# Final norm of a two-layer backbone: transposing before the root is known, and storing in half tiles

## The chip, the cores and the metric

The kernel runs on one core of a Trainium2 chip. The core has TensorE (PE, the matrix engine), VectorE (DVE), ScalarE (ACT), GpSimd (POOL) and SyncE (SP), each with its own instruction stream; they are ordered by semaphores alone. SP issues all transfers between memory (DRAM) and the on-chip SBUF. They run on 16 DMA engines. TensorE writes its results to PSUM, eight banks of 512 fp32 numbers in each of 128 partitions. The metric is the time of one execution on the device in microseconds (us).

## The reference

Two streams of tokens, 512 latent and 128 context tokens with 1024 channels each, pass through two layers (attention of several kinds, then a gated MLP). The change touches only what comes after the second layer:

```python
def rmsnorm(x, g):
    xf = x.astype(jnp.float32)
    y = xf * lax.rsqrt(jnp.mean(xf * xf, axis=-1, keepdims=True) + EPS)
    return (y * g.astype(jnp.float32)).astype(x.dtype)
...
    y_prompt = rmsnorm(xp, final_norm)
    y_sample = rmsnorm(xs, final_norm)
```

Each token's row is divided by the root of its mean square (the "root" below is the reciprocal of that root, one number per token) and multiplied by a weight per channel. Everything is fp32.

## The kernel before

The state X is kept transposed: channels on the partitions, tokens along the free dimension. X has KT = 8 tiles of 128 channels, each with T = 644 columns: 512 latent tokens, 2 zero columns, 128 context tokens, 2 zero columns. There are TT = 5 token tiles of 128, starting at the columns TILE0. The outputs have tokens as rows, so the end needs 5 x 8 transposes of 128 x 128 blocks, done on TensorE with the identity matrix (line 1149 in the profile, helper `tr`).

The order of the work is written out by hand for each engine. Semaphores count up over the whole program. The names that matter at the end of the second layer (DEPTH = 2):

- TensorE ends the MLP with the down products for channel tiles 4 to 7, each into two PSUM banks. DVE adds each to X (`add_products`, line 1699) and counts x_fin up, tile by tile. The earlier part of the residual was added to X from the buffer DN (`residual`, counted by x_pre).
- ACT squares each finished tile (`square`, line 905), DVE sums the squares over tiles into SUM (`add_square`, lines 1632 and 1635, counted by ss_add).
- `statistics` on TensorE sums SUM over the channels into five columns of bank 5 (st_mm). DVE makes the mean squares out of them (`norm_start`, line 1642, nv), POOL raises them to the power -0.5 (`norm_root`, line 847, rv). NS holds both.
- In the version before, DVE then puts each token's root on the diagonal of a tile (DG, line 1645), TensorE spreads these over all partitions into banks 6 and 7 (`spread_roots`), DVE multiplies X by them into XN (`normalise`, lines 1656 and 1657, two buffers), ACT multiplies by the norm's weight FN into YO (line 1132, counted by fin_y), TensorE transposes, and two engines copy out of PSUM into OUT: DVE the first 512 channels of a token tile (line 1604, fin_ev[0]), ACT the second 512 (line 885, fin_ev[1]). SP sends a token tile when both halves are there (line 821).

The same functions `norm_start` and `normalise` serve the four norms inside the layers.

SBUF space is reused by stages. YO and OUT lie over buffers of the MLP: CF, G_hi and G_lo take the first 12 T columns of that region, DN the 8 T behind them.

Of the kernel before, what the change touches and what calls it, by code (L numbers as in the profile page):

```python
# [17 lines left out]
F32 = mybir.dt.float32  # L18
F32R = mybir.dt.float32r
ACT = mybir.ActivationFunctionType  # L20
ALU = mybir.AluOpType
# [3 lines left out]
P = 128  # L25
D = 1024
DEPTH = 2
KT = D // P
NLAT, NCTX = 512, 128
QT = NLAT // P  # L30
CTX0 = NLAT + 2
T = CTX0 + NCTX + 2
HALF = 384
TILE0 = [P * i for i in range(QT)] + [CTX0]
TT = QT + 1
# [5 lines left out]
EPS = 1e-6  # L41
# [271 lines left out]
def backbone_program(nc, x_prompt, x_sample, cache_mla_ckv, cache_mla_kpe, cache_gqa_k, cache_gqa_v,  # L313
# [5 lines left out]
    with ctx:  # L319
        def sb(name, shape, dt=F32, stack=ctx):  # L320
            return stack.enter_context(nc.sbuf_tensor(name, shape, dt))

        def sem(name):
# [3 lines left out]
        X = sb("X", [P, KT, T])  # L327
# [10 lines left out]
        NS = sb("NS", [P, 2, 8])  # L338
        FN = sb("FN", [P, KT])
# [17 lines left out]
        t = ExitStack()  # L357
# [11 lines left out]
        XN = sb("XN", [P, 2, T], F32, b)  # L369
# [16 lines left out]
        a = ExitStack()  # L386
# [4 lines left out]
        t = ExitStack()  # L391
        KS = sb("KS", [P, TT + 1, 4, P], F32, t)
        t.close()
        t = ExitStack()
# [4 lines left out]
        t = ExitStack()  # L399
# [6 lines left out]
        a = ExitStack()  # L406
# [6 lines left out]
        a = ExitStack()  # L413
# [5 lines left out]
        a = ExitStack()  # L419
# [3 lines left out]
        AS0 = sb("AS0", [P, NAS, D], F32, a)  # L423
        a.close()
        a = ExitStack()
        YO = sb("YO", [P, KT, T], F32, a)
        OUT = sb("OUT", [P, TT, D], F32, a)
        a.close()
        b.close()

        PS = ctx.enter_context(nc.psum_tensor("PS", [P, 8, 512], F32))
# [5 lines left out]
        aw_used, x_pre = sem("aw_used"), sem("x_pre")  # L437
# [7 lines left out]
        sq_done, ss_add, st_mm, nv, rv, dg, bc_mm = (sem(n) for n in (  # L445
            "sq_done", "ss_add", "st_mm", "nv", "rv", "dg", "bc_mm"))
        xn, hf, h_hi, h_lo = sem("xn"), sem("hf"), sem("h_hi"), sem("h_lo")
# [11 lines left out]
        new_out, x_mid, x_fin = sem("new_out"), sem("x_mid"), sem("x_fin")  # L459
# [3 lines left out]
        fin_y, fin_tr, y_out = sem("fin_y"), sem("fin_tr"), sem("y_out")  # L463
        fin_ev = [sem("fin_ev_dve"), sem("fin_ev_act")]

        block = ctx.enter_context(nc.Block())

        def staged(l, x):

# [188 lines left out]
        def _(sp):  # L658
# [41 lines left out]
            for l in range(DEPTH):  # L700
# [40 lines left out]
                for r in range(NATTADA + NPROJ + NOUT):  # L741
                    kind, n = RAW_KIND[r]
# [3 lines left out]
                    elif n < NTOKEN:  # L746
                        ch, k, kn = TOKEN_ITEMS[n]
                        c0, w = TOKEN_CHUNKS[ch]
                        src = w_in[bass.ds(l, 1), P * k:P * (k + kn), c0:c0 + w]
                    elif n < NPROJ:  # L750
                        c0 = FEAT_CHUNKS[ch - NTOKEN // 2]
# [6 lines left out]
                    if kind == "w" and n >= NPROJ and kh == 1:  # L758

                        for g, a in [(g, a) for g in range(2) for a in range(2)]:  # L760
                            r0 = 512 + 256 * g + P * a
                            rows = w_out[l, r0:r0 + P, 256 * ch:256 * (ch + 1)]
                            dst = RW[HD * a:HD * (a + 1), ring(l, r), 512 * g:512 * (g + 1)]
# [51 lines left out]
                        stage_ada(l + 1, x)  # L815
            sp.wait_ge(new_out, 96 * DEPTH)
            for i in range(TT):
                sp.wait_ge(fin_ev[0], i + 1)
                sp.wait_ge(fin_ev[1], i + 1)
                dst = y_sample[0, P * i:P * (i + 1), :] if i < QT else y_prompt[0, :, :]  # L820
                sp.dma_start(dst, OUT[:, i, :]).then_inc(y_out, 16)
            sp.wait_ge(y_out, 16 * TT)

# [57 lines left out]
        def _(act):  # L883
            def copy(dst, src):
                return nc.scalar.activation(dst, src, ACT.Copy)  # L885
# [48 lines left out]
            for l in range(DEPTH):  # L934
# [21 lines left out]
                for ch in range(len(TOKEN_CHUNKS)):  # L956
# [4 lines left out]
                    dst, w = (PMG, PMM, PMS)[ch], TOKEN_CHUNKS[ch][1]  # L961
                    for i in range(TT):
# [5 lines left out]
                        if ch == 1:  # L968
                            ins = copy(dst[:, i, 0:w], of)
                        else:  # L970
                            copy(dst[:, i, 0:256].rearrange("p (j a n) -> p a j n", j=2, a=2),
                                 of[:, 0:256].rearrange("p (a j n) -> p a j n", j=2, a=2))
                            ins = copy(dst[:, i, 256:w], of[:, 256:w])
# [4 lines left out]
                for o in range(2):  # L978
                    for dst, src in zip(pieces(GC[:, o, :]), halves(o)):
                        ins = copy(dst, src)  # L980
# [142 lines left out]
                    act_pairs(m)  # L1123


            for t in range(KT):
                act.wait_ge(x_fin, DEPTH * KT + t + 1)
                square(2 * DEPTH, t)
            for t in range(KT):
                act.wait_ge(xn, 2 * DEPTH * KT + t + 1)  # L1130
                for c0, c1 in ((0, NLAT), (CTX0, CTX0 + NCTX)):
                    ins = nc.scalar.activation(YO[:, t, c0:c1], XN[:, t % 2, c0:c1], ACT.Copy,
                                               scale=FN[:, t:t + 1])
                ins.then_inc(fin_y, 1)
            for i in range(TT):
                act.wait_ge(fin_tr, TT + i + 1)
                copy(OUT[:, i, 512:D], PS[:, i, :]).then_inc(fin_ev[1], 1)

# [2 lines left out]
        def _(pe):  # L1143
# [3 lines left out]
            def tr(out, in_):  # L1147
                n = in_.shape[0]
                return nc.tensor.transpose(out, in_, K[0:n, K_ID:K_ID + n])  # L1149
# [3 lines left out]
            for i in range(TT):  # L1153
                pe.wait_ge(x_in[i], 16)
                for hb in range(2):
                    n = 2 * i + hb
                    if n >= 6:
                        pe.wait_ge(x_ev, n - 5)
                    for t in range(4):
                        ins = tr(PS[:, n % 6, P * t:P * (t + 1)], XIN[:, i, P * (4 * hb + t):P * (4 * hb + t + 1)])  # L1160
# [32 lines left out]
            def statistics(N):  # L1193

                pe.wait_ge(ss_add, N * 7 + 7)
                for i in range(TT):
                    ins = mm(PS[:, 5, i:i + 1], SUM[:, TILE0[i]:TILE0[i] + P], ONES[:, 0:1], True, True)
                ins.then_inc(st_mm, 1)

            def spread_roots(N):  # L1200

                for i in range(TT):
                    pe.wait_ge(dg, N * TT + (i + 1))
                    out = PS[:, 6, P * i:P * (i + 1)] if i < QT else PS[:, 7, 0:P]
                    ins = mm(out, ONES, DG[:, i, :], True, True)
                ins.then_inc(bc_mm, 1)
# [10 lines left out]
            for l in range(DEPTH):  # L1217
# [11 lines left out]
                for x in range(8 * ADA_A):  # L1229
                    rows, landed_, value = staged(l, x)  # L1230
# [16 lines left out]
                for s, (ch, k0, kn) in enumerate(TOKEN_ITEMS):  # L1247
                    w = TOKEN_CHUNKS[ch][1]
                    w_ready(s)
                    for kk in range(kn):  # L1250
# [3 lines left out]
                        for i in range(TT):  # L1254
# [4 lines left out]
                            c0 = TILE0[i]  # L1259
# [4 lines left out]
                            ins = mm(out, H_lo[:, k, c0:c0 + P], whi, False, k == KT - 1)  # L1264
# [4 lines left out]
                for f in range(3):  # L1269
                    for kh in range(2):  # L1270
# [6 lines left out]
                        for kk in range(4):  # L1277
                            for o in range(2):
                                pair = (o, 2 + o, o)[f]
                                ins = three(halves(pair), wslot(l, s), 2 * P * kk + P * o,  # L1280
                                            (H_hi[:, 4 * kh + kk, :], H_lo[:, 4 * kh + kk, :]),
                                            kh == 0 and kk == 0, kh == 1 and kk == 3)
# [277 lines left out]
                for t in range(4):  # L1560
                    pe.wait_ge(up_ev, l * 44 + (40 + t + 1))
                    for kc in range(2):
                        ins = gated_product(t, wslot(l, NW - 4), PAIRS % 2, kc, kc == 0, False)
                ins.then_inc(w_used, 1)
                pe.wait_ge(w_lo, l * NW + (RAW + NW - 2))
                for kc in range(2):
                    pe.wait_ge(g_lo, l * 22 + 21 + kc)
                    for t in range(4):
                        ins = gated_product(t, wslot(l, NW - 3), (PAIRS - 1) % 2, kc, False, kc == 1)
# [4 lines left out]
                for t in range(4):  # L1574
                    pe.wait_ge(x_fin, (l + 1) * KT + (t + 1))
                    for p in range(2):
                        ins = gated_products(t, wslot(l, NW - 2 + p), (PAIRS - 2 + p) % 2, p == 0, p == 1)
# [3 lines left out]
                        ins.then_inc(dn_mm, 1)  # L1581


            statistics(2 * DEPTH)
            spread_roots(2 * DEPTH)
            for n in range(2 * TT):
                hb, i = divmod(n, TT)
                if i == 0:
                    pe.wait_ge(fin_y, 4 * hb + 4)
                if hb:  # L1590
                    pe.wait_ge(fin_ev[0], i + 1)
                for t in range(4):
                    ins = tr(PS[:, i, P * t:P * (t + 1)], YO[:, 4 * hb + t, TILE0[i]:TILE0[i] + P])
                ins.then_inc(fin_tr, 1)

# [2 lines left out]
        def _(dve):  # L1600
            v = nc.vector

            def copy(dst, src):
                return v.tensor_copy(dst, src)
# [12 lines left out]
            for n in range(2 * TT):  # L1617
                dve.wait_ge(x_tr, n + 1)
                c0, hb = TILE0[n // 2], n % 2
                ins = copy(X[:, 4 * hb:4 * hb + 4, c0:c0 + P], PS[:, n % 6, :].rearrange("p (t n) -> p t n", n=P))  # L1620
# [7 lines left out]
            def add_square(N, t):  # L1628
# [4 lines left out]
                else:  # L1633
                    dve.wait_ge(ss_add, N * 7 + (t - 1))
                    v.tensor_tensor(SUM[:, :], SUM[:, :], SQ[:, t % 2, :], ALU.add).then_inc(ss_add, 1)

            def norm_start(N):

                v.memset(HF[:, :, NLAT:CTX0], 0.0)
                v.memset(HF[:, :, T - 2:T], 0.0)  # L1640
                dve.wait_ge(st_mm, N + 1)
                v.tensor_scalar(NS[:, 0, 0:TT], PS[:, 5, 0:TT], 1.0 / D, EPS, ALU.mult, ALU.add).then_inc(nv, 1)
                dve.wait_ge(rv, N + 1)
                for i in range(TT):
                    v.tensor_scalar(DG[:, i, :], IDENT, NS[:, 1, i:i + 1], None, ALU.mult).then_inc(dg, 1)
                for t in range(2):
                    normalise(N, t)

            def normalise(N, t):
                if t < 2:  # L1650
                    dve.wait_ge(bc_mm, N + 1)
                elif N == 2 * DEPTH:
                    dve.wait_ge(fin_y, t - 1)
                else:
                    dve.wait_ge(hf, N * (2 * KT) + (2 * t - 2))
                v.tensor_tensor(XN[:, t % 2, 0:NLAT], X[:, t, 0:NLAT], PS[:, 6, :], ALU.mult)  # L1656
                v.tensor_tensor(XN[:, t % 2, CTX0:CTX0 + P], X[:, t, CTX0:CTX0 + P], PS[:, 7, 0:P],
                                ALU.mult).then_inc(xn, 1)
# [44 lines left out]
            for l in range(DEPTH):  # L1703
# [36 lines left out]
                for t in range(TT):  # L1740
                    r = SS[:, 1, 6 * t:6 * t + 6].rearrange("p (h o) -> p h o", o=1).to_broadcast([P, 6, HD])
                    qk = PMG[:, t, 0:384].rearrange("p (h n) -> p h n", n=HD)
                    ins = v.tensor_tensor(qk, qk, r, ALU.mult)
# [279 lines left out]
                assert own.n == DVE_OWN, own.n  # L2023

            add_square(2 * DEPTH, KT - 1)
            norm_start(2 * DEPTH)
            for t in range(2, KT):
                normalise(2 * DEPTH, t)
            for i in range(TT):
                dve.wait_ge(fin_tr, i + 1)  # L2030
                copy(OUT[:, i, 0:512], PS[:, i, :]).then_inc(fin_ev[0], 1)


# [52 lines left out]
```

## Time and profile before

| | |
|---|---|
| Median of 3 runs | 1773.33 us (1772.14 to 1773.69) |
| Profiled execution | 1772.28 us |
| Its span | 1770.4 us |
| TensorE busy | 1676.5 us, 95% of the span |
| Last matrix product of the second layer | issued at 1742.87 us |
| First output transfer issued | 1762.18 us |
| Output | 5 transfers of 512 KB, 2.62 MB |

The span runs from the first to the last event of the core in the trace, and the execution's own time is 1.88 us longer. Times below are counted from the span's start. A timeline row names the start, the duration, the engine, the line, the operation and "out<-in" with the shapes; several of one kind in a row are merged, with their count, and the duration is that of the whole row. In brackets stands how long the engine had been idle and what ended that.

### The profile page before, as it was taken

Reading aid. Unit: us, or ns where it says so; the run is one execution under the profiler, and the core shown is the slowest. Engines: PE = TensorE matmul, PEld = TensorE weight load, DVE = VectorE, ACT = ScalarE, POOL = GpSimd, SP = SyncE. Lnnn points to the kernel's source line nnn. Section 1 sums busy time; section 2 is a strip of 40 time slices with the busy share of each in tenths; the row PEclk is TensorE's granted clock in tenths of the full one; section 3 lists DMA queues with packets and bytes.
Section 4 is the critical chain, followed back from the end, with each engine's and each line's share of the span. In section 5 each row is a group of like instructions: output and inputs, shape, how many; then the busy total and the mean of one; then the engine's idle time right before and its main releaser. Section 6 shows DMA issues by size and latency. Waiting matters only on the chain.

```text
span 1770.4 us, 29691 instructions
## 1 busy us (share of the span) xinstructions
PE 1676.5 (95%) x11702; PEld 1511.6 (85%) x11702; DVE 1011.8 (57%) x1647; ACT 597.2 (34%) x1109; POOL 542.9 (31%) x297
## 2 busy tenths in 40 slices
PE   6999998998999999999989999899799999999996
PEld 4888555798999999999968965569799999999996
DVE  4275445236766666666834744442576666666675
ACT  3423444425222222222342244452432222222223
POOL 1354010222433334333325500113233334443340
PEclk7999999998999999999999999999899999999998
DMA  8323541121222222222443245202122222222211
GB/s 320 106 72 91 169 129 38 42 67 48 78 77 71 71 71 71 74 80 72 175 149 95 60 151 154 86 25 60 37 72 73 82 72 71 71 77 77 84 48 60
DMA packets 147730, 156.17 MB, mean 88 GB/s; under 512 B 8201, under 2 KB 118325, under 8 KB 147637
## 3 DMA queue, kind: packets, MB, share of 16 engines
q1 hardware_dynamic: 147636, 154.87, 28.2%
q8 instruction: 66, 1.08, 0.3%
q14 instruction: 28, 0.22, 0.0%
HBM read 151.54 MB, written 3.31 MB: 87 GB/s over the span
## 4 chain that ended last, share of the span: by engine, by line
PE 61%; issue 20%; POOL 9%; ACT 4%; DVE 3%; DMA 1%; SPq 1%; POOLq 0%; ACTq 0%; DVEq 0%
PE PS L1145 56%; POOL W_lo L839 8%; PE PS L1149 5%; ACT HF L913 1%; ACT PT L885 1%; POOL SS L855 1%; DMA AS<-in_w_ada_dram 1%; ACT PR L1019 1%; DMA BS_N<-in_w_ada_dram 0%; ACT W_hi L885 0%; ACT H_hi L885 0%; ACT PMM L885 0%; DVE HO L1873 0%; DVE H_lo L1663 0%; DVE XN L1656 0%
## 5 line engine op out<-in xcount | busy, mean ns | idle before, releaser
L839 POOL TENSOR_TENSOR W_lo<-RW,W_hi 128x1024 fp32r<-128x1024 f32 (+1 forms) x184 | 482.6, 2632 | 939.7 <-ACT W_hi L885 939.7
L1145 PE MATMUL PS<-H_hi,W_hi 128*128 128x384 f32 x1856 | 577.6, 311 | 12.2 <-DVE H_lo L1663 7.9
L1145 PE MATMUL PS<-H_hi,W_lo 128*128 128x384 f32 x1856 | 578.1, 311 | 0.0
L1145 PE MATMUL PS<-H_lo,W_hi 128*128 128x384 f32 x1856 | 578.0, 311 | 0.0
L1145 PEld LDWEIGHTS PS<-H_hi,W_hi 128*128 128x128 f32 x1856 | 353.6, 190 | 13.6 <-issue 13.5
L1145 PEld LDWEIGHTS PS<-H_hi,W_lo 128*128 128x128 f32 x1856 | 352.1, 190 | 0.0
L1145 PEld LDWEIGHTS PS<-H_lo,W_hi 128*128 128x128 f32 x1856 | 351.9, 190 | 0.1
L885 ACT ACTIVATE W_hi<-RW 128x1024 fp32r<-128x1024 f32 (+1 forms) x184 | 191.2, 1047 | 100.6 <-PE PS L1145 100.6
L1145 PE MATMUL PS<-G_hi,W_hi 128*128 128x384 f32 x704 | 218.7, 311 | 2.2 <-DVE G_lo L1936 2.2
L1145 PE MATMUL PS<-G_lo,W_hi 128*128 128x384 f32 x704 | 218.1, 310 | 0.0
L1145 PE MATMUL PS<-G_hi,W_lo 128*128 128x384 f32 x704 | 217.9, 310 | 0.0
L885 ACT ACTIVATE U<-PS 128x384 f32<-128x384 f32 (+1 forms) x176 | 67.2, 434 | 386.0 <-PE PS L1145 385.7
L1926 DVE SCALAR_TENSOR_TENSOR CF<-U,VT,CF 128x644 f32<-128x644 f32 x88 | 189.1, 2149 | 10.2 <-DVE CF L1923 2.4
L1921 DVE TENSOR_SCALAR CF<-U,VT 128x644 f32<-128x644 f32 x88 | 51.3, 582 | 240.3 <-ACT U L885 239.8
L1923 DVE SCALAR_TENSOR_TENSOR CF<-U,VT,CF 128x644 f32<-128x644 f32 x88 | 138.8, 1577 | 10.3 <-DVE CF L1921 2.4
L1949 DVE TENSOR_TENSOR DN<-PS,DN 128x384 f32<-128x384 f32 (+1 forms) x288 | 120.9, 478 | 25.8 <-PE PS L1145 25.8
L1145 PEld LDWEIGHTS PS<-G_hi,W_hi 128*128 128x128 f32 x704 | 132.8, 189 | 2.6 <-DVE G_lo L1936 2.6
L1145 PEld LDWEIGHTS PS<-G_hi,W_lo 128*128 128x128 f32 x704 | 133.7, 190 | 0.0
L1145 PEld LDWEIGHTS PS<-G_lo,W_hi 128*128 128x128 f32 x704 | 132.6, 188 | 0.0
L885 ACT ACTIVATE G_hi<-CF 128x644 fp32r<-128x644 f32 x44 | 32.7, 744 | 238.2 <-DVE CF L1932 238.2
L1145 PE MATMUL PS<-W_hi,H_hi 128*128 128x512 f32 (+1 forms) x240 | 90.9, 379 | 9.7 <-DVE H_lo L1663 7.4
L885 ACT ACTIVATE PT<-PS 128x512 f32<-128x512 f32 (+1 forms) x102 | 53.9, 577 | 112.7 <-PE PS L1149 108.6
(188 smaller groups left out, 1901.9 us busy)
## 6 DMA issues: line engine op xcount, KB each, us to landing
RW<-in_w_up_dram SPq DMA_DIRECT2D x88, 512.0 KB, 3.7
RW<-in_w_ada_dram SPq DMA_DIRECT2D x64, 512.0 KB, 4.0
RW<-in_w_down_dram SPq DMA_DIRECT2D x44, 512.0 KB, 3.6
RW<-in_w_in_dram SPq DMA_DIRECT2D x28, 512.0 KB, 3.7
AS<-in_w_ada_dram SPq DMA_DIRECT2D x16, 512.0 KB, 11.7
RW<-in_w_out_dram SPq DMA_DIRECT2D x32, 128.0 KB, 3.0
RW<-in_w_out_dram SPq DMA_DIRECT2D x8, 512.0 KB, 3.5
BS_N<-in_w_ada_dram SPq DMA_DIRECT2D x8, 512.0 KB, 7.5
```

Of the source, the lines that this page charges most:

```text
L839: nc.gpsimd.tensor_tensor(W_lo[:, slot, 0:width], RW[:, raw, 0:width], W_hi[:, slot, 0:width].bitcast(F32), ALU.subtract).then_inc(w_lo, 1)
L855: nc.gpsimd.tensor_tensor(SS[:, 1, 0:40], SS[:, 0, 0:40], K[:, K_MH:K_MH + 40], ALU.pow).then_inc(hp, 1)
L885: return nc.scalar.activation(dst, src, ACT.Copy)
L913: nc.scalar.activation(HF[:, t % 2, c0:c1], XN[:, t % 2, c0:c1], ACT.Identity, bias=MOD[:, 24 * w + t, cond:cond + 1], scale=AB[:, w, t, c ...
L1019: nc.scalar.activation(prob_ap(step, u), score_ap(step, u), ACT.Exp, bias=stat(step, 0, u), scale=scale, accum_out=stat(step, 1, u)).then_ ...
L1145: return nc.tensor.matmul(out, lhsT, rhs, start=start, stop=stop, skip_group_check=True)
L1149: return nc.tensor.transpose(out, in_, K[0:n, K_ID:K_ID + n])
L1921: v.tensor_scalar(CF[:, ch, s, :], U[:, ch, s, 0:T], column(0), None, ALU.mult).then_inc(cv_own, 1)
L1923: v.scalar_tensor_tensor(CF[:, ch, s, :], U[:, ch, s, 1:T + 1], column(1), CF[:, ch, s, :], ALU.mult, ALU.add).then_inc(cv_own, 1)
L1926: v.scalar_tensor_tensor(CF[:, ch, s, :], U[:, ch, s, 2:T + 2], column(2), CF[:, ch, s, :], ALU.mult, ALU.add).then_inc(cv_done, 1)
L1949: ins = v.tensor_tensor(out, src, out, ALU.add)
```

## The change

The final norm is written out in another order. ACT multiplies each tile of X by the norm's weight, right after squaring it, into YO. TensorE transposes those tiles without the root: the first 512 channels of all five token tiles before `statistics`, the second 512 after it, in the banks that `final_bank` names. The root, one number per token, is applied by DVE and ACT while they copy a transposed tile (now with tokens on the partitions) out of PSUM. `spread_roots`, DG, XN and the products that filled it are gone from the final norm, and the mean squares have a function of their own, `roots`, which `norm_start` calls too. SP sends each half of a token tile by itself: ten transfers of 256 KB with rows of 2 KB in place of five of 512 KB with rows of 4 KB. YO and OUT change places in SBUF, so that YO lies over DN and OUT over CF and G_hi. ACT waits for x_pre before it writes YO.

```diff
@@ memory @@
+        OUT = sb("OUT", [P, TT, D], F32, a)
+        sb("beside_output", [P, 12 * T - TT * D], F32, a)
         YO = sb("YO", [P, KT, T], F32, a)
-        OUT = sb("OUT", [P, TT, D], F32, a)
...
+        def final_bank(hb, i):
+
+            return (6, 7, 5, 0, 1)[i] if hb else i
@@ SP @@
             for i in range(TT):
-                sp.wait_ge(fin_ev[0], i + 1)
-                sp.wait_ge(fin_ev[1], i + 1)
-                dst = y_sample[0, P * i:P * (i + 1), :] if i < QT else y_prompt[0, :, :]
-                sp.dma_start(dst, OUT[:, i, :]).then_inc(y_out, 16)
-            sp.wait_ge(y_out, 16 * TT)
+                rows = y_sample[0, P * i:P * (i + 1), :] if i < QT else y_prompt[0, :, :]
+                for hb in range(2):
+                    sp.wait_ge(fin_ev[hb], i + 1)
+                    sp.dma_start(rows[:, 512 * hb:512 * (hb + 1)],
+                                 OUT[:, i, 512 * hb:512 * (hb + 1)]).then_inc(y_out, 16)
+            sp.wait_ge(y_out, 32 * TT)
@@ ACT @@
+            act.wait_ge(x_pre, DEPTH * KT)
             for t in range(KT):
                 act.wait_ge(x_fin, DEPTH * KT + t + 1)
                 square(2 * DEPTH, t)
-            for t in range(KT):
-                act.wait_ge(xn, 2 * DEPTH * KT + t + 1)
-                for c0, c1 in ((0, NLAT), (CTX0, CTX0 + NCTX)):
-                    ins = nc.scalar.activation(YO[:, t, c0:c1], XN[:, t % 2, c0:c1], ACT.Copy,
-                                               scale=FN[:, t:t + 1])
-                ins.then_inc(fin_y, 1)
+                nc.scalar.activation(YO[:, t, :], X[:, t, :], ACT.Copy, scale=FN[:, t:t + 1]).then_inc(fin_y, 1)
+            act.wait_ge(rv, 2 * DEPTH + 1)
             for i in range(TT):
                 act.wait_ge(fin_tr, TT + i + 1)
-                copy(OUT[:, i, 512:D], PS[:, i, :]).then_inc(fin_ev[1], 1)
+                nc.scalar.activation(OUT[:, i, 512:D], PS[:, final_bank(1, i), :], ACT.Copy,
+                                     scale=NS[:, 1, i:i + 1]).then_inc(fin_ev[1], 1)
@@ TensorE @@
+            def final_rows(hb, i):
+
+                for t in range(4):
+                    ins = tr(PS[:, final_bank(hb, i), P * t:P * (t + 1)], YO[:, 4 * hb + t, TILE0[i]:TILE0[i] + P])
+                ins.then_inc(fin_tr, 1)
+            pe.wait_ge(fin_y, 4)
+            for i in range(TT):
+                pe.wait_ge(x_fin, DEPTH * KT + 5 + i // 2)
+                final_rows(0, i)
             statistics(2 * DEPTH)
-            spread_roots(2 * DEPTH)
-            for n in range(2 * TT):
-                hb, i = divmod(n, TT)
-                if i == 0:
-                    pe.wait_ge(fin_y, 4 * hb + 4)
-                if hb:
-                    pe.wait_ge(fin_ev[0], i + 1)
-                for t in range(4):
-                    ins = tr(PS[:, i, P * t:P * (t + 1)], YO[:, 4 * hb + t, TILE0[i]:TILE0[i] + P])
-                ins.then_inc(fin_tr, 1)
+            pe.wait_ge(fin_y, KT)
+            for i in range(TT):
+                if i == 2:
+                    pe.wait_ge(nv, 2 * DEPTH + 1)
+                elif i > 2:
+                    pe.wait_ge(fin_ev[0], i - 2)
+                final_rows(1, i)
@@ DVE @@
+            def roots(N):
+
+                dve.wait_ge(st_mm, N + 1)
+                v.tensor_scalar(NS[:, 0, 0:TT], PS[:, 5, 0:TT], 1.0 / D, EPS, ALU.mult, ALU.add).then_inc(nv, 1)
...
             add_square(2 * DEPTH, KT - 1)
-            norm_start(2 * DEPTH)
-            for t in range(2, KT):
-                normalise(2 * DEPTH, t)
+            roots(2 * DEPTH)
+            dve.wait_ge(rv, 2 * DEPTH + 1)
             for i in range(TT):
                 dve.wait_ge(fin_tr, i + 1)
-                copy(OUT[:, i, 0:512], PS[:, i, :]).then_inc(fin_ev[0], 1)
+                v.tensor_scalar(OUT[:, i, 0:512], PS[:, final_bank(0, i), :], NS[:, 1, i:i + 1], None,
+                                ALU.mult).then_inc(fin_ev[0], 1)
```

## Rows read from the trace of the kernel before

**Rows 1.** The page: one engine's busy time, and the DMA queue's packets.
```profile
PE 1676.5 (95%) x11702; PEld 1511.6 (85%) x11702; DVE 1011.8 (57%) x1647; ACT 597.2 (34%) x1109; POOL 542.9 (31%) x297
...
q1 hardware_dynamic: 147636, 154.87, 28.2%
```

**Rows 2.** Timeline of the end, from the last down product on.
```profile
1742.87 0.28 PE L1145 MATMUL PS<-G_hi,W_lo 128*128 128x256 f32 x1
1743.19 1.14 DVE L1699 SCALAR_TENSOR_TENSOR X<-PS,MOD,X 128x384 f32<-128x384 f32 x3 [1.68 <-PE PS L1145]
1744.24 1.75 DVE L1635 TENSOR_TENSOR SUM<-SUM,SQ 128x644 f32<-128x644 f32 x2
1744.36 0.74 ACT L905 ACTIVATE SQ<-X 128x644 f32<-128x644 f32 x1 [2.81 <-DVE X L1699]
...
1746.05 1.27 PE L1145 MATMUL PS<-K,SUM 128*128 128x1 f32 x10 [2.90 <-DVE SUM L1635]
1747.36 0.16 DVE L1642 TENSOR_SCALAR NS<-PS 128x5 f32<-128x5 f32 x1 [1.34 <-PE PS L1145]
1747.60 1.16 POOL L847 TENSOR_TENSOR NS<-NS,K 128x5 f32<-128x5 f32 x1 [19.97 <-DVE NS L1642]
1748.80 1.07 DVE L1645 TENSOR_SCALAR DG<-K,NS 128x128 f32<-128x128 f32 x5 [1.28 <-POOL NS L847]
...
1752.61 7.83 ACT L1132 ACTIVATE YO<-XN,FN 128x512 f32<-128x512 f32 x16 [7.51 <-DVE XN L1657]
...
1756.55 6.66 PE L1149 MATMUL PS<-K,YO 128*128 128x128 f32 x40 [4.90 <-ACT YO L1132]
...
1762.18 4.16 SPq L821 DMA_DIRECT2D out_dram<-OUT  x5
```

**Rows 3.** Stretches with the DMA share and GB/s last; packets of 33 to 36.
```profile
1762.60:1763.00 0.40, 0.40 (x6) 0.37 (x4) 0.00 (x0) 0.40 (x2) 0.00 (x0) 1.00 0.00 0
1763.00:1763.40 0.40, 0.21 (x2) 0.00 (x0) 0.00 (x0) 0.40 (x2) 0.00 (x0) 1.00 0.98 399
...
1769.20:1769.60 0.40, 0.00 (x0) 0.00 (x0) 0.00 (x0) 0.00 (x0) 0.00 (x0) 0.50 0.75 287
...
33.00:36.00 3.00, 2.72 (x34) 1.01 (x34) 1.77 (x5) 0.21 (x1) 0.00 (x0) 0.88 0.98 380
...
DMA packets 594, 1.14 MB, mean 380 GB/s; under 512 B 37, under 2 KB 37, under 8 KB 594
```

**Rows 4.** Groups by line and shape, ACT: a scaled and a plain copy.
```profile
L1132 ACT ACTIVATE YO<-XN,FN 128x512 f32<-128x512 f32 x8 | 5.7, 714 | 7.7 <-DVE XN L1657 7.5
...
L885 ACT ACTIVATE H_hi<-HO 128x512 fp32r<-128x512 f32 x12 | 7.6, 631 | 9.9 <-DVE HO L1873 9.9
```

**Rows 5.** Timeline of ACT and DVE while the last down products run.
```profile
1732.53 1.14 DVE L1699 SCALAR_TENSOR_TENSOR X<-PS,MOD,X 128x384 f32<-128x384 f32 x3 [0.40 <-PE PS L1145]
...
1736.09 1.14 DVE L1699 SCALAR_TENSOR_TENSOR X<-PS,MOD,X 128x384 f32<-128x384 f32 x3 [1.68 <-PE PS L1145]
...
1737.25 0.75 ACT L905 ACTIVATE SQ<-X 128x644 f32<-128x644 f32 x1 [2.81 <-DVE X L1699]
```

**Rows 6.** Stretches: length, busy PE, PEld, DVE, ACT, POOL; granted clock; DMA share, GB/s.
```profile
1743.20:1746.00 2.80, 0.00 (x0) 0.00 (x0) 2.70 (x7) 0.74 (x1) 0.00 (x0) 1.00 0.00 0
...
1756.50:1759.30 2.80, 2.75 (x13) 2.75 (x14) 2.59 (x8) 2.71 (x6) 0.00 (x0) 0.50 0.00 0
...
1761.50:1764.00 2.50, 1.71 (x16) 1.47 (x14) 0.87 (x2) 2.50 (x5) 0.00 (x0) 1.00 0.42 162
```

**Rows 7.** Instructions of the tile OUT: ns min/median/max, first and last start.
```profile
L1604 DVE COPY OUT<-PS x5: 679/679/683, 1759.3 to 1761.7; 128x512 f32<-128x512 f32 x5
L885 ACT ACTIVATE OUT<-PS x5: 592/607/632, 1761.5 to 1763.4; 128x512 f32<-128x512 f32 x5
L821 SPq DMA_DIRECT2D out_dram<-OUT x5: 356/608/1153, 1762.2 to 1765.2; - x5
...
DMA to landing us min/median/max: 2.7/4.2/4.8
```

More of the change, by code:

```diff
@@ L1640, in norm_start @@
                 v.memset(HF[:, :, T - 2:T], 0.0)
-                dve.wait_ge(st_mm, N + 1)
-                v.tensor_scalar(NS[:, 0, 0:TT], PS[:, 5, 0:TT], 1.0 / D, EPS, ALU.mult, ALU.add).then_inc(nv, 1)
+                roots(N)
                 dve.wait_ge(rv, N + 1)
@@ L1651, in normalise @@
                     dve.wait_ge(bc_mm, N + 1)
-                elif N == 2 * DEPTH:
-                    dve.wait_ge(fin_y, t - 1)
                 else:
```

## The prediction

> **What bounds the kernel now.** The page comes first. TensorE is busy for 95% of the span [rows 1], so almost everywhere only work taken off TensorE would count. The end is different, and the change lies there. The timeline of the end is read next. The last down product is issued at 1742.87 us. From there to the span's end at 1770.4 no matrix work of the layers is left, and each step waits for the one before [rows 2]. Read it as a relay. DVE adds the last residual tile (1743.19) and the last squares. TensorE sums over channels (1746.05). DVE turns the sums into mean squares (1747.36), and POOL raises them to the power -0.5 from 1747.60 for 1.16 us. Only then, at 1748.80, does the old normalisation start: the diagonal tiles DG, their spreading, 16 products on DVE beside 16 scaled copies on ACT (7.83 us from 1752.61), 40 transposes (6.66 us from 1756.55), copies out, and at 1762.18 the first output transfer. So 1762.18 - 1748.80 = 13.38 us pass between "the roots are there" and "the first byte may leave".
>
> The stretches of the DMA engines are read last. They stand at 0.00 until 1763.00, are at 0.98 right after, and are still at 0.75 in the last stretch with data, 1769.20 to 1769.60 [rows 3]. From its first issue on, the output phase is bound by bytes: 2.62 MB (5 x 128 rows x 4 KB) at 399/0.98 = 407 GB/s take 6.44 us. The issue adds 0.82 us in front, and some 0.9 us lie behind the data.
>
> **The change, part by part.** *Scaled copies moved ahead of the roots.* ACT makes YO from X itself, one copy of 644 columns per tile, each behind that tile's square. Such a copy of 512 columns takes 714 ns [rows 4]; scaled by columns this is 0.90 us at most. A tile comes every 3.55 us (DVE's adds at 1732.53 and 1736.09), and ACT sits idle for 2.81 us before a square [rows 5]. I cost the copies at nothing: that idle time hides them. For the first tiles, which come closer together, a square may end some 0.3 us later. DVE has 0.40 us of slack before the add at 1732.53 and 1.68 before the next [rows 5]. Without any cover the eight copies would cost 8 x 0.90 = 7.2 us. The new ACT wait for x_pre has only squares queued behind it, and they need tiles that DVE updates after those residuals, in program order. The last square (1744.36) stands before the last copy, so the sums keep their time. The copy ends by 1744.36 + 0.74 + 0.90 = 1746.0, before the sums over channels are done.
>
> *Twenty transposes ahead of the sums.* TensorE now transposes the first half of all five token tiles between its last product and the statistics. Their inputs (YO 0 to 3, residual tiles up to 6) are ready by then. At full clock 16 transposes took 1.71 us, 0.107 each; at half clock 13 took 2.75, 0.212 each [rows 6]. The granted clock of 1743.20 to 1746.00 is 1.00, right after products without a gap [rows 6]. So I take 0.107: 20 x 0.107 = 2.14 us from about 1743.2 to 1745.3, inside the old wait until 1746.05. Cost nothing, with 0.7 us to spare; at half clock they would end at 1747.4 and make the sums 1.4 us late. Those sums are what is queued behind them.
>
> *Second half of the transposes.* They follow the sums, from about 1747.3. Tiles 0 and 1 need no bank back, tile 2 waits for DVE's read of bank 5 (1747.52), tiles 3 and 4 for DVE's first and second copy out. Tile 3 would be ready near 1750.0 (half clock: 1750.4) and ACT gets to its fourth copy at about 1750.5: nothing, or a few tenths behind the transfers.
>
> *Taken out:* DG, its spreading, the 16 products, two clears of HF and the old copies. They are the 13.38 us. In their place stands one copy out that multiplies by the token's root. A plain DVE copy of this shape took 679 ns with starts 0.60 apart, ACT's 607 ns and 0.48 [rows 7]. The trace has no such DVE multiply that reads PSUM. Bounds: 0.68 us as the copy, and 1.07 for five multiplies of 128 columns [rows 2], which makes 1.07 x 4 / 5 = 0.86 for 512. I take 0.68, as shape and source are those of the copy. For ACT, a scale from memory makes 714 instead of 631 ns from SBUF [rows 4], so about 0.69 from PSUM. Ten halves are then ready between 1749.5 and 1751.9, 256 KB per 0.30 us, twice as fast as the engines can carry them.
>
> *First issue.* DVE starts at 1748.80 and ends at 1749.48. SP issued 0.07 us after ACT's first copy before (1761.50 + 0.61 to 1762.18), so 1749.55 instead of 1762.18: a gain of 12.63 us.
>
> *Ten half transfers.* The bytes stay and the rows become 2 KB. Stores of 2 KB rows aren't in the trace. The nearest is a load: in 33 to 36 us, 594 packets with 37 small ones carry 1.14 MB, 2 KB each, at 380 GB/s for a share of 0.98 [rows 3], 388 GB/s. The far bound is the whole queue's mean, 154.87 MB in 28.2% of the span [rows 1], 310 GB/s at 1 KB a packet. 2.62 MB take 6.76 us at 388 and 8.45 at 310, against 6.44 now: a loss of 0.3 (taken) to 2.0 us. A rule of the Trainium skill would make even this 0.3 nothing: "DMA: Bandwidth & Descriptors", Specifications, asks for only 512 B per transfer to reach line rate, so the sum would be 12.6; the rows of this trace, which differ between 2 KB and 4 KB, decide for 12.3.
>
> SP needs ten issues instead of five. One takes 356 ns at the least and 608 in the median, and the longest, 1153, belong to a full queue [rows 7]. A half needs 0.68 us of transfer and the next issue is there after 0.43 to 0.68 us (0.07 between two), so the engines stay fed, just so at the upper value. Nothing else is queued on SP. Its waits alternate between DVE's and ACT's half of a tile; both are ahead of it after the first.
>
> **The sum.** 12.63 - 0.32 = 12.3 us. The profiled execution took 1772.28 us for its span of 1770.4, so 1760.0. It lies 1.05 below the median of the runs, 1773.33, so the time to expect is 1773.33 - 12.3 = 1761.0 us.
>
> **Rivals.** *Stores of half rows are slower, or the issues limit.* For it: the queue's 310 GB/s, and issues of 0.61 us. Against it: the 2 KB loads at 388. Price 8.45 - 6.76 = 1.7 us: 1762.7.
>
> *The moved transposes hold up the sums.* The clock falls by 1743 or they start late. For it: 0.50 in 1756.50 to 1759.30, after gaps. Against it: 1.00 in the very stretch. Price 1.4 us: 1762.4.
>
> *The early copies aren't hidden.* ACT's eight copies delay squares, DVE's sums wait for squares, DVE's adds stand behind the sums, and TensorE's last products wait for freed banks. For it: that chain of waits exists. Against it: 2.81 and 1.68 us of idle time per tile. In full 7.2 us: 1768.2.
>
> *Slower than before: the ten transfers go one behind the other.* Each 256 KB would cost a whole landing, which is 2.7 us at the least for an output transfer of today [rows 7]; SP's queue is the place. End: 1749.55 + 27 + some 0.4 = 1776.95, that is 1773.33 + 6.5 = 1779.9. It decides from (12.63 + 1770.4 - 1762.18)/10 = 2.1 us per half. Against it: the five transfers of today are issued within 3.0 us [rows 7] and all their bytes pass between 1763.0 and 1769.6 [rows 3], where five landings of 2.7 us in a row would be 13.5, so they overlap. The Trainium skill speaks for this rival: "DMA: Bandwidth & Descriptors", Rules for kernel authors, asks for 1 MiB or more per DMA, and its fit of about 2.0 us fixed plus bytes at 436 GB/s makes an estimate of 2.6 us per half, 26 us in a row; that fit is for transfers issued by GpSimd, and the overlap in this trace goes against adding it up.
>
> **How the numbers follow.** Forecast 0.70, half rows 0.17, held-up sums 0.06, uncovered copies 0.04, transfers in a row 0.03. The predicted time is the forecast's, 1761.0. The three runs lie from 1.2 below to 0.4 above their median. The range starts at 1761.0 - 0.3 - 1.2 = 1759.5 (no loss by half rows) and ends at 1762.7 + 0.4 = 1763.1, which takes in the half rows and the held-up sums. What a measurement can tell from no change is about 0.2%, 3.5 us: the first three cases are faster, and the fourth in full by 5.1 us. Faster 0.95; same 0.02, for uncovered copies that also hold TensorE; slower 0.03.
>
> **What the profile will show.** Scaled copies between the squares, and DVE's adds at an unchanged pace of 3.55 us; twenty transposes of about 0.11 us behind the last product; the sums over channels starting 3.2 us after that product, as now; DVE's first copy out some 0.04 us behind POOL's root and of 0.68 us; SP's first issue 0.8 us after the root; ten issues; the DMA engines full for some 6.8 us; the end some 8.5 us after the first issue. I am wrong if the first issue comes later than 1750.5, or if the phase behind it is much over 8.5 us: by the first a relay step is new, by the second half rows cost more than 2 KB loads let me think.

## The result, and the profile after

The change took 1760.64 us in the median of four runs (1760.21 to 1761.42), against 1773.51 for the kernel before (four runs, three of them those of the table above): a ratio of 0.993 with a 95% interval of 0.9918 to 0.9942. The forecast was 1761.0. The profiled execution took 1760.21 us for a span of 1758.2, which is 12.2 us below the span before; the sum had been 12.3. Of all runs in this document one, of the kernel called "five whole again" below, took 3945.34 us; it stands in none of the medians.

The timeline of the end, to be laid beside [rows 2], names start, duration, engine, line and operation as there.

```profile
1742.79 0.28 PE L1149 MATMUL PS<-G_hi,W_lo 128*128 128x256 f32 x1
...
1742.92 2.34 PE L1153 MATMUL PS<-K,YO 128*128 128x128 f32 x20
1743.12 1.14 DVE L1711 SCALAR_TENSOR_TENSOR X<-PS,MOD,X 128x384 f32<-128x384 f32 x3 [1.68 <-PE PS L1149]
1744.17 1.75 DVE L1645 TENSOR_TENSOR SUM<-SUM,SQ 128x644 f32<-128x644 f32 x2
1744.28 0.74 ACT L911 ACTIVATE SQ<-X 128x644 f32<-128x644 f32 x1 [2.08 <-DVE X L1711]
1744.93 0.82 ACT L1136 ACTIVATE YO<-X,FN 128x644 f32<-128x644 f32 x1
...
1745.97 1.28 PE L1149 MATMUL PS<-K,SUM 128*128 128x1 f32 x10 [0.71 <-DVE SUM L1645]
...
1747.11 1.51 PE L1153 MATMUL PS<-K,YO 128*128 128x128 f32 x12
1747.29 0.16 DVE L1650 TENSOR_SCALAR NS<-PS 128x5 f32<-128x5 f32 x1 [1.37 <-PE PS L1149]
1747.53 1.17 POOL L853 TENSOR_TENSOR NS<-NS,K 128x5 f32<-128x5 f32 x1 [19.94 <-DVE NS L1650]
1748.73 3.00 ACT L1140 ACTIVATE OUT<-PS,NS 128x512 f32<-128x512 f32 x5 [2.98 <-POOL NS L853]
1748.73 3.38 DVE L2042 TENSOR_SCALAR OUT<-PS,NS 128x512 f32<-128x512 f32 x5 [1.28 <-POOL NS L853]
...
1749.54 1.32 PE L1153 MATMUL PS<-K,YO 128*128 128x128 f32 x8 [0.92 <-DVE OUT L2042]
1749.56 5.86 SPq L826 DMA_DIRECT2D out_dram<-OUT  x10
```

The relay up to POOL's root stands where it stood, 0.07 us earlier as a whole. Behind the root, everything from the diagonal tiles to the plain copies out has given way to one scaled copy: DVE and ACT start their copies at 1748.73, and SP issues at 1749.56, not 1762.18. Twenty transposes sit in the gap before the sums, which wait 0.71 us where they had waited 2.90.

The instructions of the tile OUT answer to [rows 7], the stretches to [rows 3] and [rows 6].

```profile
L826 SPq DMA_DIRECT2D out_dram<-OUT x10: 357/600/645, 1749.6 to 1754.8; - x10
L1140 ACT ACTIVATE OUT<-PS,NS x5: 682/688/705, 1748.7 to 1751.0; 128x512 f32<-128x512 f32 x5
L2042 DVE TENSOR_SCALAR OUT<-PS,NS x5: 741/741/750, 1748.7 to 1751.4; 128x512 f32<-128x512 f32 x5
...
DMA to landing us min/median/max: 2.0/3.0/3.1
```

```profile
1743.10:1745.90 2.80, 2.16 (x20) 1.92 (x18) 2.68 (x5) 1.46 (x2) 0.00 (x0) 1.00 0.00 0
...
1749.50:1750.30 0.80, 0.76 (x5) 0.53 (x6) 0.80 (x2) 0.80 (x2) 0.00 (x0) 1.00 0.00 0
...
1750.30:1757.40 7.10, 0.55 (x4) 0.31 (x4) 1.81 (x3) 1.43 (x3) 0.00 (x0) 0.59 1.00 369
...
1757.40:1757.60 0.20, 0.00 (x0) 0.00 (x0) 0.00 (x0) 0.00 (x0) 0.00 (x0) 0.50 0.01 0
```

The DMA engines are full (share 1.00) from 0.8 us behind the first issue until 0.8 us before the end. Ten transfers are issued between 1749.6 and 1754.8 and overlap. So of the phase from first issue to end, 1758.2 - 1749.56 = 8.64 us, 7.10 us are bytes, as 6.60 of the 8.22 us before were:

```profile
1763.00:1769.60 6.60, 0.21 (x2) 0.00 (x0) 0.00 (x0) 1.05 (x3) 0.00 (x0) 0.85 1.00 397
```

### The profile page after: what moved, and what is told of

It reads as the page before. It is cut to its first block, busy times and chain, and to the rows that moved or that the text cites. A ratio compares the mean times of both kernels' runs of the same rounds, so it can differ in the third digit from the quotient of the medians.

```text
span 1758.2 us, 29644 instructions
## 1 busy us (share of the span) xinstructions
PE 1672.2 (95%) x11692; PEld 1509.4 (86%) x11692; DVE 1004.4 (57%) x1624; ACT 596.0 (34%) x1101; POOL 543.4 (31%) x297
## 4 chain that ended last, share of the span: by engine, by line
PE 62%; issue 20%; POOL 9%; ACT 4%; DVE 3%; DMA 1%; SPq 1%; POOLq 0%; DVEq 0%; ACTq 0%
PE PS L1149 57%; POOL W_lo L845 8%; PE PS L1153 4%; ACT PT L891 1%; POOL SS L861 1%; DMA AS<-in_w_ada_dram 1%; ACT HF L919 1%; ACT PR L1025 1%; DMA BS_N<-in_w_ada_dram 0%; ACT H_hi L891 0%; ACT W_hi L891 0%; ACT PMM L891 0%; DVE HO L1885 0%; DVE H_lo L1675 0%; DVE CF L1935 0%
## 5 line engine op out<-in xcount | busy, mean ns | idle before, releaser
L1149 PE MATMUL PS<-H_hi,W_hi 128*128 128x384 f32 x1856 | 578.0, 311 | 12.2 <-DVE H_lo L1675 7.9
L1935 DVE SCALAR_TENSOR_TENSOR CF<-U,VT,CF 128x644 f32<-128x644 f32 x88 | 140.9, 1601 | 10.3 <-DVE CF L1933 2.4
```

What stands on the lines that cost most here:

```text
L1149: return nc.tensor.matmul(out, lhsT, rhs, start=start, stop=stop, skip_group_check=True)
L1935: v.scalar_tensor_tensor(CF[:, ch, s, :], U[:, ch, s, 1:T + 1], column(1), CF[:, ch, s, :], ALU.mult, ALU.add).then_inc(cv_own, 1)
```

## The experiments

One number serves all of them. The same work does not reach its last stage at the same instant in every execution: in the kernels whose code up to there is the same, DVE's last residual addition starts between 1741.27 and 1745.10 us. This scatter is part of every time, but not of what follows that addition: the change, measured twice, takes 15.08 and 15.01 us from there to the end. The table therefore measures from the addition's start: to the first issue, then to the span's end (the phase).

| kernel | median us (runs) | ratio to before, interval | last addition | to first issue | phase | both |
|---|---|---|---|---|---|---|
| before | 1773.51 (4) | | 1743.19 | 18.99 | 8.22 | 27.21 |
| the change | 1760.64 (4) | 0.993, 0.9918 to 0.9942 | 1743.12 | 6.44 | 8.64 | 15.08 |
| five whole transfers | 1759.85 (4) | 0.9928, 0.9909 to 0.9947 | 1741.44 | 6.43 | 8.23 | 14.66 |
| split alone | 1772.99 (10) | 0.9997, 0.9987 to 1.0007 | 1745.46 | 17.90 | 10.04 | 27.94 |
| transposes late | 1760.45 (4) | 0.9927, 0.991 to 0.9945 | 1741.50 | 6.45 | 8.55 | 15.00 |
| token halves | 1764.56 (4) | 0.9953, 0.9935 to 0.9972 | 1742.66 | 6.43 | 12.11 | 18.54 |
| copies uncovered | 1766.68 (5) | 0.9965, 0.9951 to 0.9979 | 1743.50 | 12.24 | 8.56 | 20.80 |
| quarter rows | 1762.87 (2) | 0.994, 0.992 to 0.996 | 1741.27 | 6.45 | 11.68 | 18.13 |
| even and odd | 1761.11 (2) | 0.993, 0.991 to 0.995 | 1743.99 | 6.43 | 9.28 | 15.71 |
| sums early | 1758.71 (4) | 0.9919, 0.9902 to 0.9935 | 1742.42 | 5.54 | 8.24 | 13.78 |
| sums early, zeroed | 1758.41 (5) | 0.9921, 0.9908 to 0.9933 | 1741.66 | 5.54 | 8.20 | 13.74 |
| the change again | 1761.09 (5) | 0.9935, 0.9922 to 0.9948 | 1744.09 | 6.45 | 8.56 | 15.01 |
| five whole again | 1761.07 (5) | 0.9929, 0.9916 to 0.9942 | 1745.10 | 6.43 | 8.17 | 14.60 |

The theory is the prediction's: a first issue one copy behind the root, then 0.8 us, the bytes at the rate of their row length, and 0.8 to 0.9 us behind them.

**Five whole transfers: undoing one part.** Only SP's loop goes back:

```diff
-                rows = ...
-                for hb in range(2):
-                    sp.wait_ge(fin_ev[hb], i + 1)
-                    sp.dma_start(rows[:, 512 * hb:512 * (hb + 1)], ...)
+                sp.wait_ge(fin_ev[0], i + 1)
+                sp.wait_ge(fin_ev[1], i + 1)
+                dst = ...
+                sp.dma_start(dst, OUT[:, i, :]).then_inc(y_out, 16)
```

> Everything of the change but the transfers: five of 512 KB again. Theory (first issue one copy out behind the root, then bytes at the rate of the row length): both halves of tile 0 are ready at 1749.5, so the first issue stays at 1749.56, and the phase from there to the span's end falls from 8.64 us to the 8.22 of before: time 1760.2. Rival (the half tiles are part of the gain, since the first bytes are ready sooner): first issue and end later by half a tile's transfer, 0.65 us or more: 1761.3 or more.

The first issue stays (6.43 us behind the addition) and the phase falls to 8.23 us. The stretch with data:

```profile
1748.70:1755.30 6.60, 0.47 (x4) 0.23 (x3) 1.73 (x3) 1.35 (x3) 0.00 (x0) 0.59 1.00 397
```

The engines are just as full (1.00) and carry 397 GB/s in rows of 4 KB, where the change carries 369 in rows of 2 KB. So cutting the tiles costs 0.4 us here and brings nothing: ACT's first copy ends before DVE's, and the first whole tile is ready no later than the first half.

**Split alone: the other part.** The kernel before with the new SP loop.

> The kernel before with only its output cut into ten half transfers. Theory: the first half leaves at 1760.05 instead of 1762.18, but the second still waits for ACT's first copy out at 1762.11; one half gone early (0.68 us) less the slower 2 KB rows (0.4): 0.3 us earlier, time 1773.2. Rival (smaller transfers are worth what they start earlier): 2.1 us earlier, 1771.4.

The median is 0.5 us below before, within what can be told from nothing. In this execution the sums over channels took 2.29 us, at a granted clock of 0.50, instead of 1.27, so the two kernels are best laid together at POOL's root (1750.90 here, 1747.60 before): the first issue follows after 12.46 us against 14.58, the end after 22.5 against 22.8. One half leaves 2.1 us early, and the rest waits for ACT. This theory held; nearly all of the gain comes from the other part.

**Transposes late.** All forty behind the sums, a tile's two halves together; DVE's and ACT's waits follow the new order:

```diff
-            pe.wait_ge(fin_y, 4)
+            statistics(2 * DEPTH)
+            pe.wait_ge(fin_y, KT)
             for i in range(TT):
                 pe.wait_ge(x_fin, DEPTH * KT + 5 + i // 2)
                 final_rows(0, i)
-            statistics(2 * DEPTH)
-            pe.wait_ge(fin_y, KT)
-            for i in range(TT):
                 if i == 2:
...
                 final_rows(1, i)
```

> The change, with all forty transposes behind the sums over channels, in pairs of halves. Theory: the root takes POOL from 1747.5 to 1748.7 anyway, and tile 0 is transposed by 1748.1 at full clock, so the first issue stays at 1749.56; 1760.6 if TensorE keeps its full clock, and up to 1761.5 if it falls to half after the gap before the sums (a tile then takes 1.7 us and the transfers starve a little). Rival (moving twenty transposes ahead of the sums is itself worth their 2.1 us): 1762.7.

The first issue is at 6.45 us, as in the change, and both together take 15.00. Timeline and two stretches:

```profile
1744.36 1.28 PE L1149 MATMUL PS<-K,SUM 128*128 128x1 f32 x10 [2.90 <-DVE SUM L1643]
1745.50 6.23 PE L1153 MATMUL PS<-K,YO 128*128 128x128 f32 x40
...
1747.00:1749.00 2.00, 2.00 (x11) 2.00 (x10) 1.41 (x2) 1.37 (x2) 0.08 (x1) 0.50 0.09 36
1749.00:1751.00 2.00, 2.00 (x16) 2.00 (x15) 1.29 (x2) 0.80 (x2) 0.00 (x0) 0.77 1.02 379
```

Even with the clock at half (0.50) from 1747 to 1749, the transposes stay ahead of the transfers: the DMA engines are full (1.02) right after. So placing them ahead of the sums is not what brings the gain. That they no longer need the root is enough: POOL's root and then the transfers cover them. What the place does change is the granted clock: in the change it stays at 1.00 from 1743.1 to 1751.0, here it falls to 0.50 after the gap of 2.90 us and the sums. In split alone it was at 0.50 already while the sums ran behind such a gap, and that cost 1 us. Whether the early place spares an execution this now and then was not tested.

**Token halves.** Ten transfers of 64 tokens by 4 KB rows, to tell row length from the number of issues:

```diff
+                sp.wait_ge(fin_ev[0], i + 1)
+                sp.wait_ge(fin_ev[1], i + 1)
...
-                    sp.wait_ge(fin_ev[hb], i + 1)
-                    sp.dma_start(rows[:, 512 * hb:512 * (hb + 1)],
...
+                    sp.dma_start(rows[64 * hb:64 * (hb + 1), :],
+                                 OUT[64 * hb:64 * (hb + 1), i, :]).then_inc(y_out, 16)
```

> The change with ten transfers of 64 tokens by 4 KB rows in place of 128 tokens by 2 KB. Theory (row length sets the rate): the phase from first issue to the end is 8.2 us as with five transfers, time 1760.2. Rival (ten issues cost it): 8.6 us as in the change, time 1760.6. The phase in the profile decides, since the times lie close together.

Theory and rival both missed: the phase is 12.11 us. **Even and odd** asks whether that is due to 64 rows or to half of the partitions; the slices are `hb:P:2` on both sides.

> As the run with ten transfers of 64 tokens by 4 KB rows, which had a phase of 12.1 us, but with the even and the odd token rows of a tile instead of its lower and its upper half. If half a tile was slow because it reads only one half of the partitions, the phase falls to 8.2 to 8.6 us, time 1760.2 to 1760.6; if any transfer of 64 rows is slow, it stays near 12 us, time 1764.5.

Stretches of the lower and upper halves first, then of the even and odd rows:

```profile
1753.00:1755.00 2.00, 0.00 (x0) 0.00 (x0) 0.00 (x0) 0.00 (x0) 0.00 (x0) 0.54 0.82 262
1755.00:1757.00 2.00, 0.00 (x0) 0.00 (x0) 0.00 (x0) 0.00 (x0) 0.00 (x0) 0.50 0.84 285
```

```profile
1750.40:1751.50 1.10, 1.09 (x8) 0.84 (x8) 1.10 (x2) 1.10 (x3) 0.00 (x0) 1.00 0.00 0
...
1752.00:1754.00 2.00, 0.00 (x0) 0.00 (x0) 0.99 (x2) 0.60 (x2) 0.00 (x0) 0.88 1.01 404
...
1758.30:1759.70 1.40, 0.00 (x0) 0.00 (x0) 0.00 (x0) 0.00 (x0) 0.00 (x0) 0.50 0.02 6
```

Spread over all partitions, rows of 4 KB pass at 404 GB/s although there are ten issues of 256 KB; the change, with as many issues of that size, has 379 to 385 in the middle of its transfers. So the rate does follow the row length, and a transfer of 64 neighbouring partitions pays for its partitions (262 and 285 GB/s, and engines that aren't full). The phase of even and odd, 9.28 us, still missed the 8.2 to 8.6 expected, mainly because 1.1 us lie ahead of the data and 1.4 behind it, where the change has 0.8 and 0.8. Why these two are longer is open, and so is what limits the half of the partitions.

**Quarter rows.** Twenty transfers of 128 tokens by 1 KB.

> The change with twenty transfers of 128 tokens by 1 KB rows. Theory (bytes at the rate of the row length, 310 GB/s at 1 KB by the whole queue's mean): a phase of 10.3 us from first issue to end, time 1762.3. Rival (the issues bind once they are smaller): twenty issues of 0.45 to 0.6 us make 9 to 12 us before the last landing of 2.0, a phase of 11.5 to 14, time 1763.5 to 1766. Rival (row length costs nothing): 8.2 to 8.6, time 1760.6.

The instructions of OUT, and one stretch:

```profile
L826 SPq DMA_DIRECT2D out_dram<-OUT x20: 332/445/492, 1747.7 to 1757.2; - x20
...
DMA to landing us min/median/max: 1.7/1.8/2.1
...
1752.00:1756.00 4.00, 0.00 (x0) 0.00 (x0) 0.00 (x0) 0.00 (x0) 0.00 (x0) 0.50 0.78 259
```

The engines are full for 0.78 only and each transfer lands after 1.8 us (3.0 in the change), so nothing queues there. Issues come (1757.2 - 1747.7)/19 = 0.50 us apart, and they bind: the phase is 11.68 us, as the rival on the issues had it (the theory's 10.3 missed). The median of the two runs, 1762.87 us, lies below that rival's range of times; with two runs and the scatter above it decides nothing. In the change the issues come (1754.8 - 1749.6)/9 = 0.58 us apart, but 256 KB need (7.10 us)/10 = 0.71, so there the bytes bind.

**Copies uncovered.** ACT makes the eight scaled copies behind the eighth square:

```diff
                 square(2 * DEPTH, t)
+            for t in range(KT):
                 nc.scalar.activation(YO[:, t, :], X[:, t, :], ACT.Copy, scale=FN[:, t:t + 1]).then_inc(fin_y, 1)
```

> The change with ACT's eight scaled copies behind all eight squares instead of between them, so that nothing hides them. Theory: copies of 0.82 us, started some 0.72 apart, run from 1745 to 1750.8; the twenty first transposes can start with the fourth copy at 1748.0 and TensorE's sums stand behind them, at 1750.2 at full clock and up to 1752.3 at half; the first issue moves by 4.2 to 6.4 us: 1764.9 to 1767.0. Rival (the copies' place doesn't matter, POOL's root and the transfers cover them): 1760.6.

Timeline, then a stretch:

```profile
1745.31 5.87 ACT L1137 ACTIVATE YO<-X,FN 128x644 f32<-128x644 f32 x8
...
1748.35 4.07 PE L1154 MATMUL PS<-K,YO 128*128 128x128 f32 x20 [4.89 <-ACT YO L1137]
1752.26 1.17 PE L1150 MATMUL PS<-K,SUM 128*128 128x1 f32 x10
...
1748.30:1752.40 4.10, 4.05 (x23) 4.05 (x23) 0.00 (x0) 2.89 (x4) 0.00 (x0) 0.58 0.00 0
```

The first issue moves by 12.24 - 6.44 = 5.8 us, within the 4.2 to 6.4 expected. In the change the sums over channels start 1745.97 - 1743.12 = 2.85 us behind DVE's last addition, which would be 1746.35 here. The transposes that stand before them wait for the copies until 1748.35: 2.0 us. Then TensorE, after an idle gap of 4.89 us, makes the twenty transposes at a mean clock of 0.58, in 4.07 us instead of 2.34, and the sums start at 1752.26: another 3.9 us. So with this order on TensorE the cover of the copies is worth nearly half the gain of the change. What uncovered copies would cost if the sums stood first, no run shows.

**A shorter way to the root.** With the transfers back to five, what is left to shorten is the way to the root. The last experiments let DVE add the seventh square before its last residual addition, and TensorE sum the first seven tiles' squares early and add the last tile's square into the same columns. The transposes are regrouped around these sums. From the second version, called zeroed:

```diff
+            pe.wait_ge(ss_add, 2 * DEPTH * 7 + 6)
+            mm(PS[:, 5, 0:TT], IDENT, K[:, K_MASK:K_MASK + TT], True, False)
+            last_statistics(SUM, False)
...
+            final_rows(0, 0)
+            final_rows(0, 1)
+            pe.wait_ge(sq_done, 2 * DEPTH * KT + KT)
+            last_statistics(SQ[:, (KT - 1) % 2, :], True).then_inc(st_mm, 1)
```

> The change with five whole transfers and a shorter way to the root: TensorE sums the first seven tiles' squares over channels before the last square is done, and adds the last tile's square straight into the same columns, so DVE's last addition (0.8 us) is off the path. Theory: sums end 0.9 us earlier behind the last product, the first issue comes 0.9 us earlier, and the transfers save their 0.4: time 1759.3. Rival (TensorE's extra sums and the first transposes delay the last sums): no gain over five whole transfers alone, 1760.2, or later.

The first version lacks the product with IDENT, which writes zeros into the five columns together, and marks the first product into each of the five columns as the start of a sum. Its roots for the 512 latent tokens then hold the last channel tile alone; its time is read for the order of the work. The zeroed version computes the whole norm.

> The run with early sums and five whole transfers once more, with the five columns zeroed together by one product with a zero operand before anything is added to them. Theory: DVE's last residual addition to the end of the span takes 13.8 us as in that run (15.1 in the change), time 1758.7. Rival (the place of the last sum is covered by something else): 14.7 us and 1759.8, as with five whole transfers alone.

For comparison on the same chip, the change and its version with five whole transfers were run once more:

> The change itself beside the two others on one chip. Theory: 15.1 us from DVE's last residual addition to the end, time 1760.6. Rival (the spread between chips is as large as what the two others gain): the three times can't be told apart.

> The change with five whole transfers, again with more runs. Theory: first issue where it was, phase of 8.2 us, 14.7 us from DVE's last residual addition to the end, time 1760.2, that is 0.4 below the change. Rival (half transfers win by starting on half a tile): 0.3 or more above the change.

The zeroed version's timeline:

```profile
1741.60 1.25 PE L1148 MATMUL PS<-K,SUM 128*128 128x1 f32 x10
1741.66 1.14 DVE L1721 SCALAR_TENSOR_TENSOR X<-PS,MOD,X 128x384 f32<-128x384 f32 x3 [0.75 <-PE PS L1148]
...
1742.83 0.74 ACT L910 ACTIVATE SQ<-X 128x644 f32<-128x644 f32 x1 [2.09 <-DVE X L1721]
...
1743.62 1.28 PE L1148 MATMUL PS<-K,SQ 128*128 128x1 f32 x10
...
1745.18 1.16 POOL L852 TENSOR_TENSOR NS<-NS,K 128x5 f32<-128x5 f32 x1 [19.05 <-DVE NS L1660]
```

The last sums follow the square directly, the first issue comes 5.54 us behind the addition instead of 6.44, 0.9 earlier as expected, and both together take 13.74 us, 1.3 less than the change. On one chip its five runs (1757.41 to 1759.29) lie wholly below the change's (1760.91 to 1761.34). It is faster than the change, and than the kernel before. Five whole transfers alone can't be told from the change by the times: on that chip they span 1758.21 to 1761.78, with a median of 1761.07 against 1761.09. There the phases decide, 8.17 and 8.23 against 8.56 and 8.64, and the expectation of 0.4 below the change was right only in the phase.

## Why the prediction was right

The two terms of the sum came out as 12.62 us (first issue) and 0.42 us (longer phase), so 12.2, where 12.63 and 0.32 had been set.

**The relay.** The step from root to first issue was forecast at 1749.55 and came at 1749.56, by two small errors against each other: the chain ran 0.07 us earlier, and DVE's multiply from PSUM takes 741 ns. I had taken 0.68, the lower of the bounds 0.68 and 0.86. That 12.62 met 12.63 this closely is luck; that one scaled copy stands between root and first issue is not. ACT's copy was forecast at 0.69 and took 0.688.

**The cover.** The scaled copies took 0.82 us, below the bound of 0.90, and ACT was still idle for 2.08 us before the last square. The run without cover shows that they are not free behind the last square.

**The moved transposes.** Forecast 2.14 us at full clock, from 1743.2 to 1745.3; measured 2.34, from 1742.92, at a granted clock of 1.00. "Cost nothing" was right. That the move itself brings nothing that the phase or the first issue shows was not seen in the prediction; the run with late transposes shows it. Nor did the prediction see that the first issue doesn't need the half tiles: with whole tiles it comes 6.43 us behind the addition, with halves 6.44.

**The transfers.** This is the term that was mis-sized, by little: 0.32 us for half rows, where the phases of the change and of five whole transfers differ by 0.41 (8.64 and 8.23). The loads of 2 KB rows [rows 3] let me put the rate at 388 GB/s; the stores made 369. The Trainium skill's line that 512 B suffice for line rate ("DMA: Bandwidth & Descriptors", Specifications) is not borne out: 2 KB rows lose 7% against 4 KB rows (369 to 397) at a full share. The Trainium skill's advice of 1 MiB or more per DMA ("DMA: Bandwidth & Descriptors", Rules for kernel authors) points the right way here, since ten transfers of 256 KB have a longer phase than five of 512 KB, but by 0.41 us in all; and even and odd rows show that the rate itself falls with the row and not with the transfer. The transfers overlap, so the rival with 2.7 us for each was far off, and of the runs made issues bind clearly only at quarter rows.

## What to carry to other kernels

A factor that is one number per row can wait until the rows are on the partitions: then it rides on a copy that is made anyway, and everything that doesn't need it moves into the wait for it. Before cutting a final transfer to start sooner, see whether the whole tile is ready any later; here, where bytes bind the end, shorter rows only cost. And when an improvement of a few microseconds is to be judged in a kernel of 1.8 ms, measure in the trace from the last event that both kernels share.

## What the hardware showed unexpectedly

Stores of 64 neighbouring partitions ran at 246 to 285 GB/s with the engines 0.80 to 0.95 full from 1751 to 1759 us, where even and odd partitions made 404. The Trainium skill ("DMA: Bandwidth & Descriptors", Rules for kernel authors) says of two transfers to disjoint partition halves "Don't bother — they serialize", because they share the same engines; here they were worse than no gain, with 12.11 - 8.64 = 3.5 us more of phase than half rows.

With rows of 1 KB, 128 to a transfer and nothing queued, one issue by SP took 0.33 to 0.49 us and came 0.50 us behind the one before.

Marking the start of a sum in one PSUM column made TensorE discard the sums begun in the other columns of that bank: of five columns, the four begun earlier kept only what was added after the fifth. The latent tokens' outputs of that kernel differ from the reference's by a relative 1.7147, which is what the reference's formula gives with the squares of the last channel tile alone; the context tokens, whose column was begun last, differ by 2e-6. The Trainium skill ("PSUM — Partial Sum Buffer", PSUM: the matmul accumulator) states that such a start clears the accumulate marks of the whole bank, and this run agrees.
